# A decoder step's final norm: the per-token factor applied in the copy out of PSUM, the output stored by halves

## What is computed

```python
def rmsnorm(x, g):
    xf = x.astype(jnp.float32)
    y = xf * lax.rsqrt(jnp.mean(xf * xf, axis=-1, keepdims=True) + EPS)
    return (y * g.astype(jnp.float32)).astype(x.dtype)
...
        return rmsnorm(x, norm_final), ...
```

## Time and profile before

| what | us |
|---|---|
| median of 3 runs | 1405.39 (1405.25 to 1405.69) |
| the profiled execution | 1408.01 |
| its span | 1406.3 |
| TensorE busy in the span | 1332.4 (95%) |
| VectorE / ScalarE / GpSimd busy | 642.3 / 428.8 / 122.2 |
| the last matmul of the last unit ends | at about 1376 |
| from there to the end of the span | about 30 |

### The profile page before, as it was taken

How to read it: one execution, slowest core, us unless ns; L and a number is a source line. 1 busy time by engine, 2 the same in 40 slices (tenths; PEclk the granted TensorE clock), 3 DMA queues, 4 the chain that set the end, 5 groups by cost and what they waited for, 6 DMA issues and landing times.

```text
span 1406.3 us, 26132 instructions
## 1 busy us (share of the span) xinstructions
PE 1332.4 (95%) x10580; PEld 1240.2 (88%) x10580; DVE 642.3 (46%) x1056; ACT 428.8 (30%) x662; POOL 122.2 (9%) x131
## 2 busy tenths in 40 slices
PE   5999999999999999989998999889999999999994
PEld 5999999999999999966666676488999999999993
DVE  7744422344555323366663565546544432344424
ACT  4322211222312114333445565522322311222212
POOL 1000000000152000023313000025000000000000
PEclk8999999999999999999999999989999999999997
DMA  7223322333221522247867886423233422333201
GB/s 181 81 80 84 134 75 60 90 89 105 90 90 45 165 89 89 90 129 268 299 222 271 294 279 229 153 90 90 61 90 89 134 76 60 90 89 104 76 0 64
DMA packets 195448, 172.08 MB, mean 122 GB/s; under 512 B 15409, under 2 KB 159282, under 8 KB 195378
## 3 DMA queue, kind: packets, MB, share of 16 engines
q1 hardware_dynamic: 195234, 170.63, 38.9%
q0 software_dynamic: 144, 0.52, 0.1%
HBM read 162.19 MB, written 8.93 MB: 122 GB/s over the span
## 4 chain that ended last, share of the span: by engine, by line
PE 85%; DVE 7%; issue 3%; ACT 2%; DMA 2%; SPq 1%; ACTq 0%; DVEq 0%
PE ps L1970 68%; PE ps L935 3%; PE ps L1018 2%; PE ps L713 2%; PE ps L1037 2%; PE ps L904 1%; PE ps L875 1%; ACT w_hi L2061 1%; PE ps L892 1%; DVE w_lo L2170 1%; PE ps L1004 1%; DVE rstd L2201 1%; SPq L581 1%; PE ps L831 1%; DMA out<-y_nat 0%
## 5 line engine op out<-in xcount | busy, mean ns | idle before, releaser
L1970 PE MATMUL ps<-n_hi,w_hi 128*128 128x272 f32 x1856 | 387.3, 290 | 19.0 <-DVE w_lo L2170 12.8
L1970 PE MATMUL ps<-n_hi,w_lo 128*128 128x272 f32 x1856 | 386.1, 290 | 0.0
L1970 PE MATMUL ps<-n_lo,w_hi 128*128 128x272 f32 x1856 | 384.5, 289 | 0.0
L2061 ACT ACTIVATE w_hi<-w_raw 128x2048 fp32r<-128x2048 f32 (+2 forms) x78 | 159.7, 2048 | 570.9 <-PE ps L1970 570.9
L1970 PEld LDWEIGHTS ps<-n_hi,w_hi 128*128 128x128 f32 x1856 | 294.3, 190 | 20.4 <-issue 13.1
L1970 PEld LDWEIGHTS ps<-n_lo,w_hi 128*128 128x128 f32 x1856 | 293.7, 190 | 0.0
L1970 PEld LDWEIGHTS ps<-n_hi,w_lo 128*128 128x128 f32 x1856 | 291.6, 190 | 0.0
L2170 DVE TENSOR_TENSOR w_lo<-w_raw,w_hi 128x2048 fp32r<-128x2048 f32 (+2 forms) x78 | 198.5, 2545 | 53.1 <-ACT w_hi L2061 52.7
L1970 PE MATMUL ps<-g_hi,w_hi 128*128 128x272 f32 x704 | 145.9, 288 | 1.7 <-DVE g_lo L2224 1.4
L1970 PE MATMUL ps<-g_hi,w_lo 128*128 128x272 f32 x704 | 145.7, 288 | 0.0
L1970 PE MATMUL ps<-g_lo,w_hi 128*128 128x272 f32 x704 | 145.1, 288 | 0.0
(11 more groups left out here) (322 smaller groups left out, 1289.5 us busy)
## 6 DMA issues: line engine op xcount, KB each, us to landing
w_raw<-in_ffn_w_in SPq DMA_DIRECT2D x88, 512.0 KB, 5.0
d_keys<-in_cache_k SPq DMA_DIRECT2D x128, 256.0 KB, 4.2
d_values<-in_cache_v SPq DMA_DIRECT2D x124, 256.0 KB, 4.9
w_raw<-in_w_in_mix SPq DMA_DIRECT2D x28, 512.0 KB, 4.7
w_raw<-in_ffn_w_out SPq DMA_DIRECT2D x16, 768.0 KB, 5.4
w_raw<-in_ffn_w_out SPq DMA_DIRECT2D x16, 640.0 KB, 4.7
w_raw<-in_w_out_mix SPq DMA_DIRECT2D x8, 512.0 KB, 4.9
x_nat<-in_x_prompt SPq DMA_DIRECT2D x4, 512.0 KB, 4.8
```

The source lines that it names most:

```text
L1970: mm = pe.matmul(bank(4 * j + 2 * t + s), wp, xp[:, k, s * HALF:(s + 1) * HALF], start=(k == 0 and wp is w[0] and xp is x_hi), stop=(k == ...
L2061: nc.scalar.activation(w_hi[j][:, 0:kt * UC], w_raw[j][:, 0:kt * UC], ACT.Copy).then_inc(w_hi_ready, 1)
```

## The change

The final norm's two factors are taken apart. The gain varies along the features, that is along the partitions of `xT`; the factor 1/root varies along the tokens, that is along the partitions after the transpose.

- ScalarE writes `x_gained` = `xT` times gain right behind the squares of the last four units (tiles 0 to 6); VectorE writes tile 7 behind the last addition to `sumsq`. `x_gained` replaces `yT` and does not need the factor.
- TensorE transposes tiles 0 to 5 of the first three token groups, then makes the token sums with the operands exchanged: `sumsq` is the weight and one column of ones moves, so that the sums stand one token per partition, in five columns of bank 7. The remaining transposes follow. The sample group takes the last 128 columns of `x_gained`, and its 32 tokens come out on partitions 96 to 127.
- Mean, root, reciprocal and the correcting step work on 128 x 5 (`y_ms`, `y_root`, `y_rstd`).
- ScalarE copies the left half of each group out of PSUM with `y_rstd` as its scale, VectorE the right half.
- `y_nat` has a buffer for each of the five groups, so no copy waits for a store. SyncE stores each half by itself: ten stores, in rows of 2 KB, of 256 KB (64 KB for the sample tokens).

```diff
--- before.py
+++ after.py
@@ -87,8 +87,8 @@
         o_hi = at("mix_out_hi", [P, KD, T], F32R, Z0)
         o_lo = at("mix_out_lo", [P, KD, T], F32R, Z0 + KD * ROW)
         x_nat = at("x_nat", [P, TT + 1, D], F32, Z0 + 2 * KD * ROW)
-        yT = at("yT", [P, KD, T], F32, Z0 + 2 * KD * ROW)
-        y_nat = at("y_nat", [P, 2, D], F32, RING)
+        x_gained = at("x_gained", [P, KD, T], F32, Z0 + (2 * CHUNKS[0] + KD) * ROW)
+        y_nat = at("y_nat", [P, TT + 1, D], F32, RING)
         a_n = at("ffn_a", [P, 2, HALF], F32, T0)
         b_n = at("ffn_b", [P, 2, HALF], F32, T0 + ROW)
         a_silu = at("ffn_a_silu", [P, 2, HALF], F32, T0 + 2 * ROW)
@@ -104,6 +104,7 @@
         sq = const("sq", [P, T])
         MS_AT = top[0]
         ms = const("mean_sq", [P, T])
+        y_ms, y_root, y_rstd = (at(f"y_{n}", [P, TT + 1], F32, MS_AT + 32 * i) for i, n in enumerate(("ms", "root", "rstd")))
         x_sq = [at("x_sq0", [P, KD, T], F32, Z0 + 2 * KD * ROW), at("x_sq1", [P, KD, T], F32, Z0 + 2 * CHUNKS[0] * ROW)]
         root = sq
@@ -152,10 +153,10 @@
         wf_split = sem("wf_split")
         ff_done = sem("ff_done")
         ff_ready = sem("ff_ready")
-        yt_ready = sem("yt_ready")
-        yt_done = sem("yt_done")
-        y_copied = sem("y_copied")
-        y_stored = [sem("y_stored0"), sem("y_stored1")]
+        xg_ready, xg_last = sem("xg_ready"), sem("xg_last")
+        yt_done = [sem("yt_done0"), sem("yt_done1")]
+        y_copied = [sem("y_copied0"), sem("y_copied1")]
+        y_stored = sem("y_stored")
@@ -168,6 +169,9 @@
         P_FFN[1] = P_MIX_OUT + KD // 4
         N_CONST_LOADS = 10
         N_TOK = [P] * TT + [NS]
+        LAST = slice(T - P, T)
+        Y_COLS = [slice(i * P, (i + 1) * P) for i in range(TT)] + [LAST]
+        Y_ROWS = [slice(0, P)] * TT + [slice(P - NS, P)]
         def halves(t):
@@ -1928,11 +1932,12 @@
                     load_columns(i + P_MIX_OUT, i * 2 + j, j, io["w_out_mix"], 0, KD)
             ffn_loads(P_FFN[1], io["ffn2_w_in"], io["ffn2_w_out"], False)
             for i in range(TT + 1):
-                sp.wait_ge(y_copied, 2 * (i + 1))
                 dst = y_prompt[0, i * P:(i + 1) * P, :] if i < TT else y_sample.rearrange("b t d -> (b t) d")
-                sp.dma_start(dst, y_nat[0:N_TOK[i], i % 2, :]).then_inc(y_stored[i % 2], 16)
-            sp.wait_ge(y_stored[0], 16 * ((TT + 2) // 2))
-            sp.wait_ge(y_stored[1], 16 * ((TT + 1) // 2))
+                for q in range(2):
+                    half = slice(q * 512, (q + 1) * 512)
+                    sp.wait_ge(y_copied[q], i + 1)
+                    sp.dma_start(dst[:, half], y_nat[Y_ROWS[i], i, half]).then_inc(y_stored, 16)
+            sp.wait_ge(y_stored, 16 * 2 * (TT + 1))
             mix_stores_waited(sp)
@@ -2036,18 +2041,36 @@
                     unit(i + P_MIX_OUT, j, KD, o_hi, o_lo)
             ffn(1, P_FFN[1], 2)
-            sum_squares(4, 2 * (P_FFN[1] + P_MIX_IN))
+            units = 2 * (P_FFN[1] + P_MIX_IN)
+
+            def transposes(i, q, ds_):
+                for d in ds_:
+                    mm = pe.transpose(ps[:, 2 * (i % TT) + q, (d - 4 * q) * P:(d - 4 * q + 1) * P],
+                                      x_gained[:, d, Y_COLS[i]], ident[:, :])
+                return mm
+
+            pe.wait_ge(xg_ready, 6)
+            pe.wait_ge(drained, units - 1)
+            for i in range(3):
+                if i == 2:
+                    pe.wait_ge(drained, units)
+                transposes(i, 0, range(4)).then_inc(yt_done[0], 1)
+                transposes(i, 1, range(4, 6))
+            pe.wait_ge(sumsq_ready, 4)
             for i in range(TT + 1):
-                n = N_TOK[i]
-                for q in range(2):
-                    if i >= 2:
-                        pe.wait_ge(y_copied, 2 * (i - 2) + q + 1)
-                    for d in range(4):
-                        if i == 0:
-                            pe.wait_ge(yt_ready, 4 * q + d + 1)
-                        mm = pe.transpose(ps[0:n, 2 * (i % 2) + q, d * P:(d + 1) * P],
-                                          yT[:, 4 * q + d, i * P:i * P + n], ident[:, :])
-                    mm.then_inc(yt_done, 1)
+                mm = pe.matmul(ps[:, 7, i:i + 1], sumsq[:, Y_COLS[i]], ones[:, 0:1], start=True, stop=True,
+                               skip_group_check=True)
+            mm.then_inc(ss_done, 1)
+            pe.wait_ge(xg_ready, 7)
+            pe.wait_ge(xg_last, 1)
+            for i in range(3):
+                transposes(i, 1, range(6, 8)).then_inc(yt_done[1], 1)
+            transposes(3, 0, range(4)).then_inc(yt_done[0], 1)
+            pe.wait_ge(ms_ready, 4)
+            transposes(3, 1, range(4, 8)).then_inc(yt_done[1], 1)
+            for q in range(2):
+                pe.wait_ge(y_copied[q], 1)
+                transposes(TT, q, range(4 * q, 4 * q + 4)).then_inc(yt_done[q], 1)
         @block.scalar
@@ -2112,9 +2135,14 @@
                             if c == 1 and f == 0:
                                 next_input(stage + 1, 2 * (2 * i + j))
                             if end:
-                                for d in range(4 * i + 2 * j, 4 * i + 2 * j + 2):
+                                two = range(4 * i + 2 * j, 4 * i + 2 * j + 2)
+                                for d in two:
                                     act.wait_ge(x_ready, 2 * KD + d + 1)
                                     square(1, d)
+                                for d in two:
+                                    if d < KD - 1:
+                                        nc.scalar.activation(x_gained[:, d, :], xT[:, d, :], ACT.Copy,
+                                                             scale=gains[:, 3, d:d + 1]).then_inc(xg_ready, 1)
                     p0 += KD // 4
             def next_input(stage, d0):
@@ -2152,15 +2180,13 @@
                     split_hi(P_MIX_OUT + i + 1, j, KD)
                     next_input(2, 2 * (2 * i + j))
             ffn(1, P_FFN[1], 2)
-            root_mean_square(4)
+            act.wait_ge(ms_ready, 4)
+            nc.scalar.activation(y_root[:, :], y_ms[:, :], ACT.Sqrt).then_inc(root_ready, 1)
+            act.wait_ge(rstd_step, 16)
             for i in range(TT + 1):
-                for q in range(2):
-                    act.wait_ge(yt_done, 2 * i + q + 1)
-                    if i >= 2:
-
-                        act.wait_ge(y_stored[i % 2], 16 * (i // 2))
-                    nc.scalar.activation(y_nat[0:N_TOK[i], i % 2, q * 512:(q + 1) * 512],
-                                         ps[0:N_TOK[i], 2 * (i % 2) + q, :], ACT.Copy).then_inc(y_copied, 1)
+                act.wait_ge(yt_done[0], i + 1)
+                nc.scalar.activation(y_nat[Y_ROWS[i], i, 0:512], ps[Y_ROWS[i], 2 * (i % TT), :], ACT.Copy,
+                                     scale=y_rstd[Y_ROWS[i], i:i + 1]).then_inc(y_copied[0], 1)
         @block.vector
@@ -2323,10 +2349,25 @@
                     for t in range(2):
                         input_lo(2, 4 * i + 2 * j + t)
             ffn(1, P_FFN[1], 2)
-            mean_squares(4)
-            for d in range(KD):
-                nc.vector.scalar_tensor_tensor(halves(yT[:, d, :]), halves(xT[:, d, :]), gains[:, 3, d:d + 1],
-                                               rstd[:, :, :], ALU.mult, ALU.mult).then_inc(yt_ready, 1)
+            nc.vector.tensor_scalar(x_gained[:, KD - 1, :], xT[:, KD - 1, :], gains[:, 3, KD - 1:KD], None, ALU.mult)\
+                .then_inc(xg_last, 1)
+            dve.wait_ge(ss_done, 4)
+            nc.vector.tensor_scalar(y_ms[:, :], ps[:, 7, 0:TT + 1], 1.0 / D, EPS, ALU.mult, ALU.add).then_inc(ms_ready, 1)
+            dve.wait_ge(root_ready, 4)
+            nc.vector.reciprocal(y_rstd[:, :], y_root[:, :]).then_inc(rstd_step, 1)
+            dve.wait_ge(rstd_step, 13)
+            nc.vector.tensor_tensor(y_root[:, :], y_rstd[:, :], y_rstd[:, :], ALU.mult).then_inc(rstd_step, 1)
+            dve.wait_ge(rstd_step, 14)
+            nc.vector.scalar_tensor_tensor(y_root[:, :], y_root[:, :], -0.5, y_ms[:, :], ALU.mult, ALU.mult)\
+                .then_inc(rstd_step, 1)
+            dve.wait_ge(rstd_step, 15)
+            nc.vector.scalar_tensor_tensor(y_rstd[:, :], y_root[:, :], 1.5, y_rstd[:, :], ALU.add, ALU.mult)\
+                .then_inc(rstd_step, 1)
+            dve.wait_ge(rstd_step, 16)
+            for i in range(TT + 1):
+                dve.wait_ge(yt_done[1], i + 1)
+                nc.vector.tensor_scalar(y_nat[Y_ROWS[i], i, 512:D], ps[Y_ROWS[i], 2 * (i % TT) + 1, :],
+                                        y_rstd[Y_ROWS[i], i:i + 1], None, ALU.mult).then_inc(y_copied[1], 1)
         @block.gpsimd
```

## The result

| | before | changed |
|---|---|---|
| first comparison, four executions each, median us | 1405.54 | 1387.88 (1384.33 to 1391.56) |
| ratio in it, 95% interval | | 0.9867 [0.9832, 0.9902] |
| ratios of two later comparisons | | 0.9877 [0.9857, 0.9897], 0.9885 [0.9855, 0.9914] |
| all executions, mean us (number, standard deviation) | 1406.33 (51, 2.52) | 1389.83 (16, 3.89) |
| profiled execution, us; its span | 1408.01; 1406.3 | 1389.80; 1388.1 |

Over all executions the change is worth 1406.33 - 1389.83 = 16.5 us, with an error of about 1.0 (2.52/sqrt(51) and 3.89/sqrt(16) added in squares). The forecast was 16.2. The first four executions of each kernel had it at 1405.39 x (1 - 0.9867) = 18.7, which is 1386.7 us and 0.9 under the low end of the range; their median, 1387.88, lies just inside it.

A forecast was written before the change was run, and what follows sets the result against it. TensorE carries 85% of the chain, untouched, so the 30.35 us tail decides: 12.54 us from (b) and 3.62 from (c), none from (a), take the median from 1405.39 to 1389.2 us; range 1387.6 to 1391.4.

The forecast's parts named there:

- The frame: Whole kernel: only the tail, from the last unit's last matmul to the span's end, changes; 16.2 us less.
- Piece (a): Last unit's end to the token sums' start (1379.21 us): early copies and 18 transposes fit into waits; change 0, bound +0.6.
- Piece (b): Token sums' start to first store: sums, narrow factor, copies from PSUM; first store at 1382.05, not 1394.59, 12.54 us earlier.
- the bound of 1.2: Upper bound in us for the five token-sum matmuls, the old four's time; 0.9 was taken.
- The clock: TensorE's granted clock during sums and transposes: expected at 1.00 up to the transposes' end.
- now it works most of that time: Reason given for the clock staying up: TensorE, hardly busy there before, now works most of the time around the sums.
- The table load: ScalarE's load for the root begins about 1378.7, ends 1380.0 before the mean, with 0.3 us of cover left.
- that rival: Root's table late: a 2.66 us switch frees ScalarE at 1381.4, not 1380.0; time 1390.2 us; chance 0.06.
- Piece (c): First store to span's end: ten stores bound by the DMA engines, 6.1 us for the bytes; gain 3.62 us.
- The fetch: Rival: a 16 KB instruction fetch among the stores adds 0.86 us on one DMA engine; 1390.1 us; chance 0.27.
- The fixed cost: Rival on stores: some 2.0 us per transfer, not overlapped, gives back 10 of 16 us; 1399.2 us; in series, not slower: 0.02.

The follow-up runs named there:

- whole_rows: Changed kernel with one store per token group in 4 KB rows, five in place of ten; tail 14.54 us, ratio 0.9884 [0.9863, 0.9904].
- after_again: The changed kernel repeated without an edit; last unit ended at 1380.43 us, tail 14.47 us.
- after_more: The changed kernel repeated without an edit for more executions; last unit ended at 1376.01 us, tail 14.49 us.
- two_buffers: Changed kernel with two output buffers again, so copies from the third group on wait for stores to land; tail 16.12 us.
- quarters: Changed kernel with each half stored as two quarters, 20 stores in rows of 1 KB; tail 17.67 us.
- late_transposes: Changed kernel with no transpose ahead of the token sums, all 40 behind them; tail 14.49 us.

## Why the prediction held, and where it did not

**The frame.** That the tail alone changes, by 16.2 us: 15.6 were measured on the tail and 16.5 on all executions. That the forecast lies only 0.3 from the latter is partly luck: it was 0.6 too high for the tail, and the 0.9 of the rest belongs to nothing that it priced. The step that failed is the term at which the range put the work ahead of the tail. It took the body's end (1375.95) as fixed and put only the tail's costs into its width. The runs showed it anywhere from 1367.7 to 1380.4, with the time of one kernel from 1381.7 to 1396.7, so 1387.6 to 1391.4 was too narrow: with four executions of each kernel the difference has an error of 2.3 us (2.52 and 3.89, each over sqrt(4), added in squares), and the 18.7 of the first comparison lies 2.2 from the 16.5 of all. That is chance, and a range that gave the body's wander no width could not hold it. The three executions shown before lay within 0.44 us of each other and gave no warning; three was too few.

**Piece (a).** Right: twelve transposes at 1373.15, the other six and `x_gained` where they were put, nothing delayed: the sums begin 3.28 us after the last unit, 3.26 before. (Two copies of 0.7 us fit into ScalarE's 12.36 us of idleness almost nine times, not ten, which changes nothing.)

**Piece (b).** Forecast 12.54, measured 18.64 - 6.66 = 11.98 (mean of three). The mis-sized terms: the sums took 1.27 to 1.57 against 0.9, over the bound of 1.2 too, because each such product is two instructions: the sum set five matmuls of the code against four instructions of the trace, which are two in the code (x4 in the earlier trace rows). VectorE's half took 0.745 against 0.68, since I had taken a row without a pointer operand; at 128x544 the same operation takes 557 ns with two such operands and 435 with none. The narrow steps were priced right: 0.21 for the root, 0.20 for the reciprocal with its hand-over, and 0.17 for each of the other four.

**The clock.** I expected 1.00 up to the end of the transposes. It fell during the sums in the first profile (0.50 at 1378) and in whole_rows, just behind them in after_again and after_more, and only after the transposes in two_buffers and quarters. The step that failed is "now it works most of that time": TensorE was busy 0.69 and 0.40 in the windows at 1375 and 1376. It cost the sums up to 0.3 us (1.57 against 1.27), and the slow transposes behind them cost nothing that shows: in late_transposes all forty stand there and the tail is the same.

**The table load.** It had 1.03 us of cover (ends 1377.33, VectorE's mean ends at 1378.36), more than the forecast 0.3, as the sums came later. The root began 2.34 us after the load's start here, 2.06 in after_again (load at 1383.16, root at 1385.22), right behind the mean each time, so a switch takes no more than 2.06. Elsewhere in the changed kernel, ScalarE alternates between two table sets:

```profile
564.94 1.28 ACT L2176 ACT_TABLE_LOAD   x1
566.23 0.66 ACT L2176 ACTIVATE mix_projT<-mix_projT  x1
```

The next activation starts 0.01 after the load's 1.28. The Trainium skill ("ScalarE: Activation LUTs", What ACT_TABLE_LOAD costs) has 2.66 us with the drain for a switch; this trace shows 1.29 from the load's start to the next activation, so that rival had no ground here.

**Piece (c).** Forecast 8.09 for the phase of stores, measured 7.90 to 7.93; gain 3.65 (from the mean of the two profiles before) against 3.62. The issues took 0.58 and not 0.47, but quarters shows that this was waiting. The fetch didn't fall among the stores: one 16 KB packet came in the window at 1378 (0.07 of the DMA engines, 16 GB/s), before them. The Trainium skill ("DMA: Bandwidth & Descriptors", Measured) advises 1 MiB or more for each transfer, beside figures for loads issued from GpSimd; here 256 KB stores from SyncE back to back kept the engines full at 369 to 389 GB/s, and 128 KB stores did not (268). The fixed cost is not paid per store where stores overlap: ten landed 2.1 to 3.1 us after their issues, and all ten were issued in 5.83.

**What I had not asked.** Five buffers, both engines and the stores by halves are worth 3.2 us together, the buffers 1.5 of it, the early transposes nothing that shows. My sum had them in piece (b) without a price of their own, as work done early, and the bytes hide that wait anyway.

## What to carry to other kernels

Where a norm's factor belongs to one axis and its gain to the other, put each where it is a per-partition scalar: the factor's arithmetic shrank from 544 columns to five, the multiplication by it went into the copy that was there anyway, and that alone was 12.4 of 15.6 us. Once output stores keep the DMA engines full, work ahead of them is worth only what moves the first store, so price each part against that. And before a range is drawn, find out how far the unchanged part wanders from one execution to the next: here one kernel's executions ranged over 15 us, four times the 3.8 us of the range.

## What the runs showed of the hardware that was not expected

- The granted clock of TensorE can fall while the engine is fully busy: 0.72 in the window at 1377 and 0.50 at 1378, both with 1.00 us busy of 1.00, after windows busy 0.69 and 0.40. In quarters and two_buffers the same sequence of work stayed at 1.00 until the transposes were done, and in after_again it fell only behind the sums.
- A one-column fp32 matmul with a new 128x128 weight costs 0.26 us, as two instructions (ten in 1.28 us in two_buffers, at 1.00).
- Stores of 128 KB (and four of 32) cost SyncE's queue 0.48 us each on average, so 20 of them for 2.23 MB hold the rate at about 268 GB/s, while stores of 256 KB reach 369 to 389.
- Executions of the changed kernel differ by up to 15 us (1381.7 to 1396.7), and the granted clock over the whole span goes with it (0.985 in the execution of 1384.33, 0.975 in that of 1396.73).
